# Hybrid encoder block on one Trainium2 core: latent attention takes its maxima over three PSUM banks at once and splits key tiles in pairs

## The chip, the cores and the metric

The kernel runs on 1 core of one Trainium2 chip. The metric is the device time of one execution in microseconds (us), median of the runs shown. Engines are called as in the profile: PE (matrix multiply) and PEld (its weight loads), ACT (ScalarE), DVE (VectorE), POOL (GpSimd), SP (issues most DMAs).

## What is computed

One encoder layer over two groups of 1040 tokens (1024 and 16 meta tokens), width 1024. Two attention mixers run in parallel on the same normed input: a grouped one (8 query heads, 2 key heads, 64 wide) and a latent one (8 heads, queries and keys 96 wide, values 64 wide). Their outputs are merged by sigmoid gates, then comes an expert-choice SwiGLU mixer. The part of the reference that the change touches:

```
def attend_mla(qb):
    qn, qr = qb[..., :MLA_NOPE_DIM], qb[..., MLA_NOPE_DIM:]
    s = (jnp.einsum('bqhd,bkhd->bhqk', qn, k_nope, preferred_element_type=jnp.float32)
         + jnp.einsum('bqhd,bkd->bhqk', qr, k_rope, preferred_element_type=jnp.float32)) * scale_m
    p = jax.nn.softmax(s, axis=-1).astype(v_m.dtype)
    o = jnp.einsum('bhqk,bkhd->bqhd', p, v_m)
...
mixed = (jax.nn.sigmoid(g_a) * jnp.matmul(o_g, w_o_gqa)
         + jax.nn.sigmoid(g_b) * jnp.matmul(o_m, w_o_mla))
h = h + jnp.matmul(mixed, w_out)
```

## The kernel before

The program is one fixed order of instructions per engine, held together by semaphores. Its stages follow one another: projections, grouped attention (`grouped_attention`), latent attention (`latent_attention`), `mix`, `residual`, choosing, experts. Every product is made of float32 operands split into a high part (a cast to float32r) and a low part (the value minus the cast), three matmuls per product.

Latent attention has 16 units (8 heads times 2 groups, unit n in program order). A unit is 3 blocks of 348, 348 and 344 queries, a block is 9 key tiles: eight of 128 keys and one of meta keys. That makes 48 blocks and 432 tiles, numbered t, with kk the tile inside its block. Per tile:

- PE, `scores(t)`: three matmuls into one of two banks of `n_st_ps` (lines 1872, 1873, 1876). Row 96 of the queries holds the maximum of each query and row 96 of the keys holds -1, so that the third matmul subtracts the maximum. The first tile of a block therefore waits in its third matmul for `row_done`.
- ACT, `exponential(t)` (L1929) writes `n_exps`, `hi(t)` (L1942, for meta keys L1937) casts it to `n_p_hi`.
- DVE, `lo(t)` (L2002, meta L1998) subtracts: `n_p_lo`.
- PE, `values(t)`: three matmuls into `n_o_ps` (L1893 to L1895), for meta keys one (L1889). They run LAG = 3 tiles behind the scores.

The maxima run ahead of all that. For each block 9 pieces are made: three chunks of 116 queries times three stretches of 348, 348 and 344 keys. A piece is one PE matmul (L1852) into one of three banks of `n_max_ps`, one DVE reduction (L1983) into `t_piece_max`; after the ninth, one or two small reductions (L1989) give `t_row_max`. One piece is issued per tile, 12 pieces ahead. In tile 7 of a block PE transposes the three columns of the next block's maxima into one row (`max_rows`, L1861), and ACT casts that row into the queries (`max_row`, L1947). ACT's order around a block's border is:

```
for t in range(NT + 1):
    if t < NT:
        exponential(t)
    if t >= 1:
        hi(t - 1)
    b, kk = tile_of(t)
    if kk == LAG + 1 and b >= 1:
        evacuate(b - 1)
    if kk == TILES - 1 and b + 1 < NB:
        max_row(b + 1)
```

When a block is finished, ACT copies its bank into `n_sums` (`evacuate`, L1957). When a unit is finished, POOL runs a chain on it: a DMA gathers the row of sums (`n_total`, L2037), DVE inverts it (`invert`, L2007, in DVE's order at tile 10 of the next unit), two DMAs spread the result (L2039, L2041), then POOL multiplies (L2043), casts (L2046) and subtracts (L2048) on 64 by 1040 elements, and two DMAs store to `o_t` (L2051). SP loads queries, keys and values of the next unit once the scores of the unit before are through; in the last unit SP waits for the store of unit 14 (`stored`), then loads the last token pieces and the first weights of `mix` (L301, L305, L308).

Between grouped and latent attention stand functions that the first leaves to the second in a dictionary `rest` (the last block's values on PE, its evacuation on ACT, its sum on DVE). POOL ends the grouped part with the scaling of its last two blocks (L1687 to L1701) and then sets row 96 of the keys with two memsets (L2029); PE waits for them (`ones_ready`) before the first scores. At the other border, `mix` begins with the cast of its first two weight pieces (ACT L2188), their subtraction (DVE L2239) and then matmuls (L2168, L2175); its SP part waits for the last unit's store (`attended["stored"]`) after the second pair of pieces.

## Time and profile before

| | before |
|---|---|
| median of 3 runs | 3044.73 us (3035.55 to 3045.96) |
| profiled execution, its own time | 3038.07 us |
| its span, first to last instruction | 3036.0 us |
| PE busy, share of the span | 2811.9 us, 93% |
| DVE busy | 1915.6 us, 63% |
| ACT busy | 1481.9 us, 49% |
| POOL busy | 628.7 us, 21% |
| mean granted PE clock | 0.968 |
| latent attention: first and last scores matmul (L1876) start | 895.8 and 1448.8 us |

A row of the time view reads: start in us, duration in us, engine, line, operation, output and inputs with shapes, count of merged instructions, and in brackets the idle time before and what ended it. Matmuls overlap: one row lasts about 0.32 us while the next starts some 0.16 us after it. Durations of groups are in ns.

### The profile page before, as it was taken

How to read it: one execution, taken by the hardware profiler on the slowest of the kernel's cores; microseconds unless marked ns; L12 is line 12 of the kernel's file. 1: busy time of each engine (PE TensorE's matmuls, PEld its weight loads, DVE VectorE, ACT ScalarE, POOL GpSimd, SP SyncE). 2: the span in 40 equal slices, each digit the busy share in tenths (PEclk: the TensorE clock that was granted, in tenths of full speed). 3: DMA queues.
4: the chain of work that ended last, by engine and by line, in shares of the span. 5: the costliest groups of instructions: out<-in, count | busy, mean ns of one | idle time of the engine just before them, and what ended most of it. 6: DMA issues, size and time to landing. Idle time of an engine off the chain costs nothing. (4 is left out here: it accounts for less than half of the span.)

```text
span 3036.0 us, 55157 instructions
## 1 busy us (share of the span) xinstructions
PE 2811.9 (93%) x19748; PEld 2615.8 (86%) x19748; DVE 1915.6 (63%) x3430; ACT 1481.9 (49%) x2813; POOL 628.7 (21%) x847
## 2 busy tenths in 40 slices
PE   8999899999989899999799999999973999999994
PEld 7888698999978788887799999988863999999994
DVE  6777667888878888888333434433335555555565
ACT  4333337888867676667322223322112445445453
POOL 0000113444431322223100000000004233333331
PEclk9999899999999999999999999999986999999997
DMA  6555592202223333452848484556646888899877
GB/s 210 159 158 181 174 370 65 71 22 71 50 45 78 86 90 88 96 141 71 252 124 243 111 242 127 146 167 188 195 128 154 191 202 200 205 207 209 196 173 263
DMA packets 534415, 466.66 MB, mean 154 GB/s; under 512 B 61906, under 2 KB 467106, under 8 KB 534256
## 3 DMA queue, kind: packets, MB, share of 16 engines
q1 hardware_dynamic: 510768, 403.68, 46.9%
q0 software_dynamic: 21120, 60.81, 9.1%
q8 instruction: 87, 1.43, 0.2%
q14 instruction: 72, 0.59, 0.1%
q10 hardware_dynamic: 2368, 0.16, 0.0%
HBM read 320.29 MB, written 144.21 MB: 153 GB/s over the span
## 5 line engine op out<-in xcount | busy, mean ns | idle before, releaser
L2168 PE MATMUL c_acc<-c_tokens,c_w_hi 128*128 128x260 f32 x2048 | 373.3, 284 | 13.1 <-DVE c_w_lo L2239 11.5
L2168 PEld LDWEIGHTS c_acc<-c_tokens,c_w_hi 128*128 128x128 f32 x2048 | 316.9, 189 | 13.5 <-issue 11.7
L2769 PE MATMUL e_gu<-e_x_hi,w_hi 128*128 128x260 f32 x1024 | 293.6, 287 | 0.9 <-DVE e_x_lo L2974 0.9
L2168 PE MATMUL c_acc<-c_tokens,c_w_lo 128*128 128x260 f32 x1024 | 289.8, 283 | 0.0
L2769 PE MATMUL e_gu<-e_x_lo,w_hi 128*128 128x260 f32 x1024 | 289.7, 283 | 0.0
L2239 DVE TENSOR_TENSOR c_w_lo<-c_raw,c_w_hi 128x1536 fp32r<-128x1536 f32 x64 | 114.5, 1790 | 277.4 <-ACT c_w_hi L2188 277.4
L2769 PE MATMUL e_gu<-e_x_hi,w_lo 128*128 128x260 f32 x1024 | 289.5, 283 | 0.0
L1929 ACT ACTIVATE n_exps<-n_st_ps 128x348 f32<-128x348 f32 (+3 forms) x432 | 198.8, 460 | 167.5 <-PE n_st_ps L1876 165.3
L2969 DVE TENSOR_TENSOR w_lo<-w_raw,w_hi 128x2048 fp32r<-128x2048 f32 x90 | 206.4, 2293 | 102.1 <-ACT w_hi L2870 101.3
L2002 DVE TENSOR_TENSOR n_p_lo<-n_exps,n_p_hi 128x348 fp32r<-128x348 f32 (+1 forms) x384 | 240.4, 626 | 38.0 <-ACT n_p_hi L1942 28.7
L1983 DVE TENSOR_REDUCE t_piece_max<-n_max_ps 116x1 f32<-116x348 f32 (+3 forms) x432 | 219.9, 511 | 41.3 <-PE n_max_ps L1852 39.7
L2188 ACT CAST c_w_hi<-c_raw 128x1536 fp32r<-128x1536 f32 x64 | 94.8, 1480 | 264.9 <-DMA c_raw<-in_w_o_gqa 228.4
L2769 PEld LDWEIGHTS e_gu<-e_x_hi,w_hi 128*128 128x128 f32 x1024 | 193.6, 189 | 1.1 <-DVE e_x_lo L2974 1.1
L2769 PEld LDWEIGHTS e_gu<-e_x_lo,w_hi 128*128 128x128 f32 x1024 | 193.7, 189 | 0.0
L2168 PEld LDWEIGHTS c_acc<-c_tokens,c_w_lo 128*128 128x128 f32 x1024 | 193.7, 189 | 0.0
L2769 PEld LDWEIGHTS e_gu<-e_x_hi,w_lo 128*128 128x128 f32 x1024 | 193.4, 189 | 0.0
L2175 PE MATMUL c_acc<-c_tokens,c_w_hi 128*128 128x260 f32 x1024 | 187.2, 283 | 0.0
L1942 ACT CAST n_p_hi<-n_exps 128x348 fp32r<-128x348 f32 (+1 forms) x384 | 181.3, 472 | 0.0
L2870 ACT CAST w_hi<-w_raw 128x2048 fp32r<-128x2048 f32 x90 | 171.2, 1902 | 8.9 <-PE e_dn L2794 7.5
L3110 POOL DMA_INDIRECT h_rows<-e_y,e_rows_out x60 | 104.9, 1748 | 333.2 <-DVE e_y L2996 319.4
L1576 DVE TENSOR_REDUCE t_peak<-t_s_ps 128x1 f32<-128x1024 f32 x132 | 160.6, 1217 | 19.7 <-PE t_s_ps L1390 19.4
L1601 DVE TENSOR_TENSOR t_pt_lo<-t_tp,t_pt_hi 128x512 fp32r<-128x512 f32 (+1 forms) x264 | 166.5, 670 | 2.3 <-ACT t_pt_hi L1522 2.0
(338 smaller groups left out, 7835.9 us busy)
## 6 DMA issues: line engine op xcount, KB each, us to landing
c_raw<-in_w_in SPq DMA_DIRECT2D x64, 512.0 KB, 5.4
w_raw<-in_w_gate SPq DMA_DIRECT2D x64, 512.0 KB, 6.7
w_raw<-in_w_up SPq DMA_DIRECT2D x64, 512.0 KB, 8.2
w_raw<-in_w_down SPq DMA_DIRECT2D x64, 512.0 KB, 4.7
c_tokens<-hn_t SPq DMA_DIRECT2D x16, 1040.0 KB, 8.9
c_tokens<-o_t SPq DMA_DIRECT2D x32, 520.0 KB, 6.7
r_mt<-mix_t SPq DMA_DIRECT2D x32, 512.0 KB, 5.2
mix_t<-c_out_hi SPq DMA_DIRECT2D x32, 260.0 KB, 2.1
```

Of the source, the lines that this page charges most:

```text
L1576: dve.tensor_reduce(peak[0:r, b % 2, i:i + 1], s_ps[0:r, n % 2, :], AX_X, ALU.max).then_inc(peak_done, 1)
L1601: dve.tensor_tensor(pt_lo[span], tp[:, f % RING, :].rearrange("p (t n) -> p t n", t=4)[:, :, 0:r], pt_hi[span].bitcast(F32), ALU.subtract) ...
L1929: act.activation(exps[0:r, t % EXPS, 0:w], st_ps[0:r, t % 2, 0:w], ACT.Exp).then_inc(exp_done, 1)
L1942: act.copy(p_hi[:, ring_slot(t), 0:w], exps[:, t % EXPS, 0:w]).then_inc(hi_done, 1)
L1983: dve.tensor_reduce(piece_max[0:r, b % 2, c, j:j + 1], max_ps[0:r, n % MAXES, 0:WIDTHS[j]], AX_X, ALU.max)\
L2002: dve.tensor_tensor(p_lo[:, at, 0:w], exps[:, t % EXPS, 0:w], p_hi[:, at, 0:w].bitcast(F32), ALU.subtract)\
L2168: pe.matmul(acc[:, b, mixer, 0:W], w[:, parity, mixer, k, :], tokens[t % 2][:, part, k, cols], start=(k == 0 and at == 0), stop=(k == DK - ...
L2175: ins = pe.matmul(acc[:, b, 2 + mixer, 0:W], w[:, parity, mixer, DK + k, :], tokens[t % 2][:, part, DK + mixer * OK + k, cols], start=(k = ...
L2239: dve.tensor_tensor(w_lo[:, parity, mixer, :, :], raw[:, mixer, :, :], w_hi[:, parity, mixer, :, :].bitcast(F32), ALU.subtract).then_inc(p ...
L2769: ins = pe.matmul(gu[:, j % 2, a, 0:W], w[:, j, at:at + P], t[:, k, :], start=(k == 0 and q == 0), stop=(k == DK - 1 and q == 2))
L2870: act.copy(w_hi[:, j, :], raw[:, j % RAW, :]).then_inc(slab_hi, 1)
L2969: dve.tensor_tensor(w_lo[:, j, :], raw[:, j % RAW, :], w_hi[:, j, :].bitcast(F32), ALU.subtract)\
```

## The change

In `latent_attention`:

- Maxima: each chunk of 116 queries is one step. Three matmuls of 348 keys (stretches from 0, 346 and 692, overlapping by two keys) fill the three banks, and one DVE reduction over 116 x 3 x 348 elements writes `t_row_max` directly. `t_piece_max` and the small reductions are gone. The next chunk's matmuls wait until the reduction before is done. The steps stand at fixed tiles: chunk 0 of block b+2 in tile 7 of block b, chunks 1 and 2 of block b+1 in tiles 1 and 3.
- The transposes of the maxima move from tile 7 to tile 6, and ACT's cast of the row from behind tile 8's exponential and tile 7's cast to directly behind tile 7's exponential.
- The cast to the high part and the subtraction handle two key tiles at once (128 x 2 x 348); the meta tile stays alone. The rings hold three pairs (before: six tiles of `n_p_hi` and four of `n_exps`).
- LAG is 5. `evacuate` stands at tile 5, without a cast beside it, and `invert` at tile 7 of the next unit.
- Border to grouped attention: the first block's chunks of maxima stand between the parts of the last grouped values; POOL's memsets stand ahead of the last grouped scaling; ACT's first row cast stands behind the last grouped evacuation.
- Border to `mix`: the last unit's inversion stands behind the subtraction of the first two weight pieces.

The diff, cut:

```diff
@@ grouped_attention @@
-            def finish():
-                for part in PARTS:
-                    values(BLOCKS - 1, part)
-                scale_rows(BLOCKS - 1)
-            rest["tensor"] = finish
+            rest["tensor"] = lambda part: values(BLOCKS - 1, part)
+            rest["parts"] = PARTS
+            rest["scale_rows"] = lambda: scale_rows(BLOCKS - 1)
...
-            for b in (BLOCKS - 2, BLOCKS - 1):
-                scale(b)
-                split_hi(b)
-                split_lo(b)
+            def finish():
+                for b in (BLOCKS - 2, BLOCKS - 1):
+                    scale(b)
+                    split_hi(b)
+                    split_lo(b)
+            rest["gpsimd"] = finish
@@ latent_attention @@
-    AHEAD, LAG = 12, 3
-    MAXES, RING, EXPS = 3, 6, 4
+    LAG = 5
+    PAIRS = XCH // 2
+    GROUPS_OF = PAIRS + 1
+    RING, EXPS = 3, 3
+    MAXIMA_AT = {7: (2, 0), 1: (1, 1), 3: (1, 2)}
...
-                if n >= MAXES:
-                    pe.wait_ge(max_done, n - MAXES + 1)
-                pe.matmul(max_ps[0:r, n % MAXES, 0:WIDTHS[j]], q[p][0:QK_M, at:at + r],
-                          k[0:QK_M, p, 0, STARTS[j]:STARTS[j] + WIDTHS[j]], start=True, stop=True).then_inc(max_filled, 1)
+                at_least(pe, max_done, 3 * b + c)
+                for j in range(3):
+                    ins = pe.matmul(max_ps[0:r, j, 0:WIDE], q[p][0:QK_M, at:at + r],
+                                    k[0:QK_M, p, 0, KEY_STARTS[j]:KEY_STARTS[j] + WIDE], start=True, stop=True)
+                ins.then_inc(max_filled, 1)
...
-            for n in range(9):
-                maxima(n)
-            grouped["rest"]["tensor"]()
-            for n in range(9, AHEAD):
-                maxima(n)
+            for c, part in enumerate(grouped["rest"]["parts"]):
+                maxima(0, c)
+                grouped["rest"]["tensor"](part)
+            grouped["rest"]["scale_rows"]()
+            maxima(1, 0)
             max_rows(0)
...
                     scores(t)
-                    if t + AHEAD < NT:
-                        maxima(t + AHEAD)
-                    if kk == TILES - 2 and b + 1 < NB:
+                    for ahead, c in chunks_at(t):
+                        maxima(ahead, c)
+                    if kk == 6 and b + 1 < NB:
                         max_rows(b + 1)
...
-                act.copy(p_hi[:, ring_slot(t), 0:w], exps[:, t % EXPS, 0:w]).then_inc(hi_done, 1)
+                act.copy(p_hi[:, ring_slot(t)[0], :, 0:w], exps[:, group % EXPS, :, 0:w]).then_inc(hi_done, 1)
...
-            for t in range(NT + 1):
-                if t < NT:
-                    exponential(t)
-                if t >= 1:
-                    hi(t - 1)
-                b, kk = tile_of(t)
-                if kk == LAG + 1 and b >= 1:
-                    evacuate(b - 1)
-                if kk == TILES - 1 and b + 1 < NB:
-                    max_row(b + 1)
+            for t in range(NT):
+                b, kk = tile_of(t)
+                exponential(t)
+                if kk == 7 and b + 1 < NB:
+                    max_row(b + 1)
+                if kk >= 2 and kk % 2 == 0:
+                    hi(t - 1)
+                if kk == 0 and b >= 1:
+                    hi(t - 1)
+                if kk == LAG and b >= 1:
+                    evacuate(b - 1)
+            hi(NT - 1)
...
-                dve.tensor_reduce(piece_max[0:r, b % 2, c, j:j + 1], max_ps[0:r, n % MAXES, 0:WIDTHS[j]], AX_X, ALU.max)\
-                    .then_inc(max_done, 1)
+                dve.tensor_reduce(row_max[0:r, b % 2, c:c + 1], max_ps[0:r, :, 0:WIDE], AX_XY, ALU.max).then_inc(max_done, 1)
...
+            for t in range(NT):
+                b, kk = tile_of(t)
+                for ahead, c in chunks_at(t):
+                    peaks(ahead, c)
+                if kk >= 2 and kk % 2 == 0:
+                    lo(t - 1)
+                if kk == 0 and b >= 1:
+                    lo(t - 1)
+                if b % BLOCKS == 0 and kk == 7 and b >= BLOCKS:
+                    invert(b // BLOCKS - 1)
+            lo(NT - 1)
...
                 pool.wait_ge(ones_ready[0], held.PREPARED + 1 + p)
+            grouped["rest"]["gpsimd"]()
             for landed, value in grouped["stored"]:
@@ mix @@
             split_pieces(0, 0, 0)
+            attended["invert_last"](dve)
```

How the change moves the instructions, at three places. First ACT around the border between two blocks inside latent attention (`t_q1_2440` are the queries with their row of maxima). Before:

```order
L1929 ACTIVATE n_exps<-n_st_ps 128x348
L1942 CAST n_p_hi<-n_exps 128x348
L1929 ACTIVATE n_exps<-n_st_ps 80x348
L1942 CAST n_p_hi<-n_exps 128x348
L1947 CAST t_q1_2440<-n_row_ps 1x348
L1929 ACTIVATE n_exps<-n_st_ps 128x348
L1937 CAST n_p_meta<-n_exps 80x348
```

and now:

```order
L1963 CAST n_p_hi<-n_exps 128x696
L1949 ACTIVATE n_exps<-n_st_ps 128x348
L1968 CAST t_q1_2440<-n_row_ps 1x348
L1949 ACTIVATE n_exps<-n_st_ps 80x348
L1963 CAST n_p_hi<-n_exps 128x696
L1949 ACTIVATE n_exps<-n_st_ps 128x348
L1958 CAST n_p_meta<-n_exps 80x348
```

The cast of the row stood behind the exponential of the block's last tile (80x348) and one more cast; it now stands ahead of both.

Second, DVE over one block that holds a unit's inversion, with the last meta subtraction of the block before as first row. Now:

```order
L2017 TENSOR_TENSOR n_p_meta<-n_exps,n_p_meta 16x344
L2008 TENSOR_REDUCE t_row_max<-n_max_ps 116x1
L2021 TENSOR_TENSOR n_p_lo<-n_exps,n_p_hi 128x696
L2008 TENSOR_REDUCE t_row_max<-n_max_ps 116x1
L2021 TENSOR_TENSOR n_p_lo<-n_exps,n_p_hi 128x696 x2
L2008 TENSOR_REDUCE t_row_max<-n_max_ps 116x1
L2026 RECIPROCAL n_inverse<-n_total 65x16
L2021 TENSOR_TENSOR n_p_lo<-n_exps,n_p_hi 128x696
L2017 TENSOR_TENSOR n_p_meta<-n_exps,n_p_meta 16x348
```

Before, a block had nine reductions of 116x348 and eight subtractions of 128x348 in turn, and the inversion stood one block later than here, behind the first subtraction:

```order
L1998 TENSOR_TENSOR n_p_meta<-n_exps,n_p_meta 16x348
L1983 TENSOR_REDUCE t_piece_max<-n_max_ps 116x1
L2002 TENSOR_TENSOR n_p_lo<-n_exps,n_p_hi 128x348
L2007 RECIPROCAL n_inverse<-n_total 65x16
L1983 TENSOR_REDUCE t_piece_max<-n_max_ps 116x1
```

Third, POOL at the border between the two attentions. Before, the memsets of `t_k` close the grouped scaling:

```order
L1687 TENSOR_TENSOR t_summed<-t_summed,t_scales 64x320
L1696 CAST t_out_hi<-t_summed 64x320
L1701 TENSOR_TENSOR t_out_lo<-t_summed,t_out_hi 64x320
L2024 UNCONDITIONAL_BRANCH
L2029 MEMSET t_k 1x1040 x2
```

and now they stand ahead of the scaling of the last two blocks:

```order
L2044 UNCONDITIONAL_BRANCH
L2049 MEMSET t_k 1x1040 x2
L1685 TENSOR_TENSOR t_summed<-t_summed,t_scales 64x384
L1694 CAST t_out_hi<-t_summed 64x384
L1699 TENSOR_TENSOR t_out_lo<-t_summed,t_out_hi 64x384
L1685 TENSOR_TENSOR t_summed<-t_summed,t_scales 64x320
```

## Rows read from the trace of the kernel before

**Rows 1.** One line's instructions (L1876): count, min/median/max ns, first and last start

```profile
L1876 PE MATMUL n_st_ps<-t_q,t_k x432: 316/323/493, 895.8 to 1448.8; 97*128 97x348 f32 x96, 97*128 97x344 f32 x48
```

**Rows 2.** Order of time, PE, a tile without a wait and the transposes

```profile
1201.76 0.32 PE L1872 MATMUL n_st_ps<-t_q,t_k 96*128 96x344 f32 x1
...
1202.85 0.32 PE L1872 MATMUL n_st_ps<-t_q,t_k 96*128 96x344 f32 x1
...
1203.32 0.32 PE L1852 MATMUL n_max_ps<-t_k,t_q 96*116 96x348 f32 x1
...
1203.71 0.39 PE L1893 MATMUL n_o_ps<-n_p_hi,t_v 128*65 128x344 f32 x1
```

**Rows 3.** Order of time, PE, two block borders that follow each other

```profile
1099.94 0.43 PE L1876 MATMUL n_st_ps<-t_q,t_k 97*128 97x348 f32 x1 [0.43 <-ACT t_q L1947]
...
1110.68 0.42 PE L1876 MATMUL n_st_ps<-t_q,t_k 97*128 97x348 f32 x1 [0.43 <-ACT t_q L1947]
```

**Rows 4.** Order of time, DVE, POOL and PE while POOL finishes a unit

```profile
1119.52 2.73 DVE L2002 TENSOR_TENSOR n_p_lo<-n_exps,n_p_hi 128x348 fp32r<-128x348 f32 x1 [0.18 <-ACT n_p_hi L1942]
...
1123.25 2.59 POOL L2048 TENSOR_TENSOR n_o_lo<-n_sums,n_o_hi 64x1040 fp32r<-64x1040 f32 x1
...
1124.01 2.21 DVE L1998 TENSOR_TENSOR n_p_meta<-n_exps,n_p_meta 16x348 fp32r<-16x348 f32 x1
...
1126.27 0.37 PE L1889 MATMUL n_o_ps<-n_p_meta,t_v 80*65 80x348 f32 x1 [1.34 <-DVE n_p_meta L1998]
```

**Rows 5.** The page's groups: busy us, mean ns of one, idle before

```profile
L2239 DVE TENSOR_TENSOR c_w_lo<-c_raw,c_w_hi 128x1536 fp32r<-128x1536 f32 x64 | 114.5, 1790 | 277.4 <-ACT c_w_hi L2188 277.4
...
L2002 DVE TENSOR_TENSOR n_p_lo<-n_exps,n_p_hi 128x348 fp32r<-128x348 f32 (+1 forms) x384 | 240.4, 626 | 38.0 <-ACT n_p_hi L1942 28.7
...
L2188 ACT CAST c_w_hi<-c_raw 128x1536 fp32r<-128x1536 f32 x64 | 94.8, 1480 | 264.9 <-DMA c_raw<-in_w_o_gqa 228.4
...
L1576 DVE TENSOR_REDUCE t_peak<-t_s_ps 128x1 f32<-128x1024 f32 x132 | 160.6, 1217 | 19.7 <-PE t_s_ps L1390 19.4
```

**Rows 6.** Order of time, border from grouped to latent attention

```profile
881.19 2.76 PE L1852 MATMUL n_max_ps<-t_k,t_q 96*116 96x348 f32 x6 [0.84 <-DVE t_piece_max L1983]
...
889.07 0.44 ACT L1947 CAST t_q<-n_row_ps 1x348 fp32r<-1x348 f32 x1 [8.52 <-PE n_row_ps L1861]
...
893.03 1.98 POOL L2029 MEMSET t_k<- 1x1040 f32 x2
...
895.06 0.66 PE L1872 MATMUL n_st_ps<-t_q,t_k 96*128 96x348 f32 x1 [6.03 <-POOL t_k L2029]
```

**Rows 7.** Order of time, from the last unit's first scores to the first matmul of mix

```profile
1416.60 0.33 PE L1872 MATMUL n_st_ps<-t_q,t_k 96*128 96x348 f32 x1
...
1423.60 0.55 POOL L2037 DMA_DIRECT2D n_total<-n_sums  x1 [11.22 <-ACT n_sums L1957]
...
1431.67 0.54 POOL L2039 DMA_DIRECT2D inverse_t<-n_inverse  x1 [7.52 <-DVE n_inverse L2007]
...
1448.40 2.08 SPq L301 DMA_DIRECT2D c_tokens<-o_t  x4
...
1463.00 0.77 PE L2168 MATMUL c_acc<-c_tokens,c_w_hi 128*128 128x260 f32 x2 [11.50 <-DVE c_w_lo L2239]
```

**Rows 8.** One tile's instructions (`n_total`): its DMA from issue to landing

```profile
DMA to landing us min/median/max: 2.4/3.5/5.2
```

**Rows 9.** Order of time, DVE, SP, ACT and PE in the first passes of mix

```profile
1457.46 0.25 DVE L2007 RECIPROCAL n_inverse<-n_total 65x16 f32<-65x16 f32 x1 [6.38 <-DMA n_total<-n_sums]
...
1477.45 1.30 SPq L301 DMA_DIRECT2D c_tokens<-hn_t  x2
...
1486.02 0.41 SPq L305 DMA_DIRECT2D c_raw<-in_w_in  x1
...
1494.46 1.48 ACT L2188 CAST c_w_hi<-c_raw 128x1536 fp32r<-128x1536 f32 x1 [9.94 <-DMA c_raw<-in_w_o_gqa]
...
1501.09 0.50 PE L2168 MATMUL c_acc<-c_tokens,c_w_hi 128*128 128x260 f32 x2 [1.56 <-DVE c_prod L2245]
```

More of the change, by code:

```diff
@@ L1760, in chunk, with groups_until, pair_before, group_end @@
         return cols.start + c * ROWS, r
[L1762 to L1764 removed]
+    def groups_until(t):
+        b, kk = tile_of(t)
+        return GROUPS_OF * b + kk // 2
     def ring_slot(t):
         b, kk = tile_of(t)
[L1769 to L1771 removed]
+        return (PAIRS * b + kk // 2) % RING, kk % 2
+    def pair_before(t):
         b, kk = tile_of(t)
[L1774 to L1775 removed]
+        x = PAIRS * b + kk // 2 - RING
+        return None if x < 0 else TILES * (x // PAIRS) + 2 * (x % PAIRS) + 1
+    def group_end(g):
+        b, j = g // GROUPS_OF, g % GROUPS_OF
+        return TILES * b + min(2 * j + 1, XCH)
+    def chunks_at(t):
+        b, kk = tile_of(t)
+        if kk in MAXIMA_AT:
+            ahead, c = MAXIMA_AT[kk]
+            if b + ahead < NB:
+                return [(b + ahead, c)]
+        return []
     with ExitStack() as ctx:
@@ L1784, in latent_attention @@
         q, k, v = held.q, held.k, held.v
[L1785 removed]
+        row_max = held.row_max
         sums = sb("sums", [VD + 1, 2, TOK])
```

101 lines of the change are left out of this document (42 added, 59 removed).

## The prediction, written before the changed kernel ran

> **What bounds the kernel now.** I read the page's forty slices first: PE is busy nearly throughout, and latent attention is a stretch in which it is a little less so, while DVE is at its highest there. Next the instructions of the scores line: 432 tiles between 895.8 and 1448.8, 1.283 us each [rows 1], so a block of nine tiles takes 11.55 us. Then the time view for what a tile must cost: between two first score matmuls with seven matmuls and no wait lie 1.09 us, 0.156 each [rows 2]. A block has 61 matmuls (27 scores, 9 maxima, 25 values), 9.55 us. The transposes of the maxima push the next value matmul from 0.16 to 0.39 us behind, 0.23 more [rows 2]. So **PE needs 9.8 us a block** and takes 11.55: 1.75 us are waits. Two quiet block borders that follow each other stand 10.74 us apart, and at each the third score matmul waited for ACT's cast of the row of maxima [rows 3]. That puts **about 0.95 us a block on this one wait** (0.43 idle by the row, the rest in the weight load held up with it and in the refill of the pipe). Units of three blocks really take (1416.60 - 895.06) / 15 = 34.8 us [rows 6, 7] against 3 x 10.74 = 32.2: **2.6 us a unit** are something else. Rows 4 show what: while POOL multiplies and subtracts 64 by 1040 elements, DVE's subtractions last 2.73 and 2.21 us, even one of 16 partitions, and the value matmul waits.
>
> **Part 1: the row of maxima comes early.** ACT now casts it behind tile 7's exponential. The exponential of tile 8 and a cast stood ahead of it before, and the first scores needed it one tile later; now there are over 1.5 tiles. The 0.95 us go if nothing on the new path is late, so I time a block, starting at its first score matmul, with tiles of 0.94 us (six matmuls), 0.47 more for the maxima in tiles 1, 3 and 7, and the transposes in tile 6. Results of a matmul are there some 0.2 us after the next could start. Durations: a pair's subtraction lies between one single and the 1536-wide one, 1790 ns [rows 5]. Less 696 against 1536 elements at DVE's 1.04 ns each (the 1024-wide reduction, 1217 ns, fits that slope) gives **0.9 us**. A three-bank reduction is the 1024-wide one plus 20 elements, **1.24 us** [rows 5]. A pair's cast is 1480 ns [rows 5] less 840 elements, between 0.67 (all proportional) and 0.94; I take 0.77.
> - Tiles 0 and 1: scores of tile 2 end at 2.8, ACT's exponential and pair cast at 4.15, DVE's subtraction at 5.05; the values want it at 5.8. Spare 0.75.
> - Chunk 1's maxima leave PE at 1.9, its reduction waits for DVE until 2.2 and ends at 3.4; PE wants the banks at 3.8. Spare 0.4. Chunk 2's reduction ends at 6.25, the transposes want it at 6.75. Spare 0.5.
> - Pairs 2-3, 4-5, 6-7 have 1.0 to 1.4 spare, the meta tile 3.
> - DVE's sum is 3 x 1.24 + 4 x 0.9 + 0.5 (a single one by the same slope) = 7.8 us, ACT's 12 of at most 0.46 (its 348-wide cast of the row: 0.44 [rows 6]) and 4 of 0.77, 8.6 us, both below 9.8.
>
> The nine small PE matmuls of maxima cost the same in threes; two keys more per chunk are nothing. Nine waits and eight small reductions that go cost nothing now, since DVE is not the bound; the cover is PE. **Gain 3 x 0.95 = 2.9 us in each of the 15 units that end before the last one starts: 43 us.**
>
> **Part 2: POOL's hold on DVE stays.** The unit's POOL work, some 6.3 us from about 1119.5 to 1125.84 [rows 4], is unchanged. By the timetable the first long one meets pair 4-5, which has 1.4 us spare and is late by little. The second meets pair 6-7, with up to 2.6 us to sit out against 1.1 spare: 1.5 us, then 0.7 at the next maxima, whose banks DVE frees late. That is 2.2 us, with 2.6 before by the sum above. LAG = 5 gives longer cover, but a pair is two tiles late at once. **I count 0.** From below: all 2.6 x 15 = 39 us gained, if the cover holds. From above: see the third rival. `invert` now stands where DVE may arrive before the data. The last block's copy ends some 7 us into a unit (its DMA starts at 1423.60, 7.0 after the unit's 1416.60 [rows 7]), its DMA lands 3.5 later, 2.4 to 5.2 [rows 8], so at 9.4 to 12.2; DVE is there at 10.2. The pair queued behind it is ready at 10.7 and has 1.1 spare, so the median costs nothing and the slowest landing about 1 us. The chain behind it starts some 3.5 us sooner: 11.3 us into the unit against 1431.67 - 1416.60 less POOL's 0.3, 14.8.
>
> **Part 3: the first border.** Scores start at 895.06 because POOL's memsets end the grouped scaling [rows 6]. Ahead of the scaling they wait only for the last grouped scores, and are done long before the 889 that comes next. Next in line is ACT's row of maxima, 889.07 to 889.5 before, and the 2.76 us in which PE ran six maxima against DVE's reductions [rows 6] shrink as values fill them. With the reductions of 1.24 us each still felt once or twice, I get first scores at 887: **8 us gained**. At least 5.5 (row as late as before), at most 9.
>
> **Part 4: the last border.** Mix starts when unit 14 is stored: 1431.67 to 1448.40 is 16.7 us, and from there weights, cast and subtraction take 14.6 to 1463.00 [rows 7]. Both stay. With the inversion 3.5 us sooner in the unit, mix starts 3.5 us sooner counted from the last unit's start, **3.5 us gained**; PE just idles longer there, since the unit's own blocks are faster too. But the last inversion now comes behind the first two weight subtractions, 2.5 us after mix's start instead of 5.5 before it (1457.46) [rows 9]. SP stands behind that store with the next tokens and the third pair of pieces: store seen 20 us after the inversion (1477.45), pieces issued at 1486.02, cast at 1494.46, PE already waits 1.56 at 1501.09 [rows 9]. In the new order the store is seen 19.5 to 22.5 after mix's start instead of 14.5. SP waited anyway some 3 us for the first output in between. So the third pieces come 2 to 5 us later: **3.6 us lost**.
>
> **Sum.** 43 + 0 + 8 + 3.5 - 3.6 = 51 us. Everything behind mix follows PE and its own weights, and moves along. The profiled execution took 3038.07 us, which becomes 2987; it lay 6.7 below the median 3044.73, which becomes **2994**.
>
> **A page that speaks against it.** Rows 4 show DVE held for most of a POOL instruction. The Trainium skill, page "SBUF — State Buffer", section "Who interferes with whom", says that a VectorE instruction with two SBUF inputs and a GpSimd instruction that reads SBUF shut each other out for the whole instruction, the later one waiting. By that rule POOL's cast holds DVE too, and fewer, longer subtractions would be hit as hard as many short ones; the trace agrees for the two arithmetic ones (2.73 and 2.21), and its rows don't isolate the cast.
>
> **Rivals.**
> 1. *The cover holds* (0.20). PE's five tiles of lag and a DVE that is busy 7.8 of 9.8 us hide POOL too. For it: three of four pairs have 1 us or more spare. Against: up to 2.6 us to sit out. It gives 51 + 25 to 39, median 2955 to 2969.
> 2. *A new short wait in each block* (0.17). The three places with 0.4 to 0.75 spare are each gone if crossing the third bank costs DVE some 0.3 us or the pair cast takes its upper bound of 0.94, and PE waits for DVE instead of ACT. It would take 0.5 to 0.9 us a block back: 24 to 43 us, median 3018 to 3037. For it: single semaphore hops are not in my timetable. Against: the 1024-wide reduction crosses two banks at 1217 [rows 5].
> 3. *POOL's work stands on PE in full* (0.07), slower. All of POOL's 6.3 us a unit end up as PE waits, because a held pair delays the reduction behind it, that the single-buffered banks, and those the transposes, each long hold with another 0.7. It costs 7.7 us a unit instead of 2.6, 77 us in 15 units, and the sum turns to 26 slower: 3071. It decides from 2.6 + 51/15 = 6 us a unit. Against: 1.1 to 1.4 us of each hold are covered by the timetable, and DVE got a subtraction through between POOL's instructions (2.73 from 1119.52, the next of 2.21 only from 1124.01 [rows 4]).
> 4. *The change doesn't reach PE* (0.06): the wait for the row is replaced by one for the exponentials, whose order on ACT got bursts of cast and copy (tiles 5 to 8 hold 4.2 us of ACT work against 4.5 of PE). Then only the border's 8 us remain, 3037.
>
> **Chances.** The forecast has 0.50, and 2975 to 3015 as its own range. The range takes in rival 1 and most of rival 2: **2960 to 3030**. It leaves out the ends of rival 1 and 2, and rivals 3 and 4. A measurement of this kernel tells some 0.5%, 15 us, from no change. Faster by more: forecast, rival 1, most of rival 2, 0.83. Within: the rest of rival 2 and rival 4, 0.10. Slower: 0.07.
>
> **What would show it.** Right: scores from about 887; 10 us between block borders in quiet stretches; no PE wait on `t_q`; single waits of PE for `n_p_lo` and `n_max_ps`, 2 to 3 us a unit; unit starts 32 us apart; pair subtractions of 0.9 us, up to 3.4 under POOL; reductions of 1.24; an idle PE of some 12 to 14 us ahead of mix, and a wait of 4 to 7 us for its third pieces. Wrong: PE waits in every block for `t_row_max` or `n_p_lo` (rival 2), for ACT's `n_exps` (rival 4), or units still 35 us apart.

## The result

| | before | after |
|---|---|---|
| median | 3042.47 us (3035.55 to 3047.84, 8 runs) | 3019.0 us (3007.32 to 3030.13, 8 runs) |
| ratio | | 0.9923 [0.9903, 0.9943] |
| profiled execution, its own time | 3038.07 us | 3020.98 us |
| its span | 3036.0 us | 3018.7 us |
| latent attention: last unit's first scores minus first scores | 521.5 us | 508.9 us |
| mean granted PE clock of the span | 0.968 | 0.965 |

The change gives 23 us by the medians, 17.3 by the two spans, and not the forecast 51: the time is inside the range of 2960 to 3030, 25 us above the 2994. In the profiles the 17.3 split up as follows, each from the start of a row (units count from 0, so U15 is the last one; "mix" is the first matmul of the output mix):

| stretch | before | after | gained | forecast |
|---|---|---|---|---|
| up to the first scores | 895.06 | 885.63 | 9.4 | 8 |
| first scores to U15 | 521.5 | 508.9 | 12.6 | 43 + 0 |
| U15 to mix | 46.4 | 42.7 | 3.7 | 3.5 |
| mix to the end | 1573.0 | 1581.4 | -8.4 | -3.6 |

So the first border and the start of the mix did about what was forecast. Most of the missing gain is in the second row (30.4 us), a smaller part in the fourth (4.8).

### The profile page after: what moved, and what is told of

Same layout as the page of the kernel before. It is cut to its first block and busy times, and to the rows that moved or that the text cites. A ratio compares the mean times of both kernels' runs of the same rounds, so it can differ in the third digit from the quotient of the medians.

```text
span 3018.7 us, 53994 instructions
## 1 busy us (share of the span) xinstructions
PE 2810.1 (93%) x19748; PEld 2624.4 (87%) x19748; DVE 1857.1 (62%) x2886; ACT 1452.7 (48%) x2621; POOL 633.6 (21%) x847
## 5 line engine op out<-in xcount | busy, mean ns | idle before, releaser
L2189 PE MATMUL c_acc<-c_tokens,c_w_hi 128*128 128x260 f32 x2048 | 375.2, 285 | 17.5 <-DVE c_w_lo L2260 9.2
L2021 DVE TENSOR_TENSOR n_p_lo<-n_exps,n_p_hi 128x696 fp32r<-128x696 f32 (+1 forms) x192 | 214.2, 1117 | 105.3 <-ACT n_p_hi L1963 104.4
L2008 DVE TENSOR_REDUCE t_row_max<-n_max_ps 116x1 f32<-116x1044 f32 x144 | 178.6, 1241 | 11.5 <-PE n_max_ps L1869 9.7
```

What stands on the lines that cost most here:

```text
L2008: dve.tensor_reduce(row_max[0:r, b % 2, c:c + 1], max_ps[0:r, :, 0:WIDE], AX_XY, ALU.max).then_inc(max_done, 1)
L2021: dve.tensor_tensor(p_lo[:, at, :, 0:w], exps[:, group % EXPS, :, 0:w], p_hi[:, at, :, 0:w].bitcast(F32), ALU.subtract).then_inc(lo_done, 1)
L2189: pe.matmul(acc[:, b, mixer, 0:W], w[:, parity, mixer, k, :], tokens[t % 2][:, part, k, cols], start=(k == 0 and at == 0), stop=(k == DK - ...
```

## The profile after

The single instructions take about what was forecast. The scores line (L1894) waits for ACT's row of maxima 2 times in all, 0.7 us. The weights' subtraction in the mix, the pairs' subtractions and the reductions have these groups on the page (busy us, mean ns of one, idle before; against [rows 5]):

```profile
L2260 DVE TENSOR_TENSOR c_w_lo<-c_raw,c_w_hi 128x1536 fp32r<-128x1536 f32 x64 | 112.6, 1759 | 290.9 <-ACT c_w_hi L2209 290.9
...
L2021 DVE TENSOR_TENSOR n_p_lo<-n_exps,n_p_hi 128x696 fp32r<-128x696 f32 (+1 forms) x192 | 214.2, 1117 | 105.3 <-ACT n_p_hi L1963 104.4
...
L2008 DVE TENSOR_REDUCE t_row_max<-n_max_ps 116x1 f32<-116x1044 f32 x144 | 178.6, 1241 | 11.5 <-PE n_max_ps L1869 9.7
```

The three-bank reduction takes 1241 ns as forecast (1.24). A pair's subtraction has a mean of 1117 ns, with 880 for an undisturbed one (below): the rest is time in which POOL held it.

Order of time after, the border into latent attention, against [rows 6]: the memsets are early, and the first scores matmul waits for nothing any more.

```profile
876.89 1.98 POOL L2049 MEMSET t_k<- 1x1040 f32 x2
...
885.63 0.40 PE L1890 MATMUL n_st_ps<-t_q,t_k 96*128 96x348 f32 x1
```

The windows view shows where a unit's time goes. The rows are two quiet blocks and the third of unit 4, a quiet one and the third of unit 6, and the third of unit 9, each from its first scores (L1890) to the next block's: length, busy us of each engine with instructions, granted PE clock (as a share of 2.4 GHz), DMA share and GB/s.

```profile
1029.01:1039.04 10.03, 10.03 (x67) 9.36 (x65) 7.50 (x9) 7.52 (x17) 0.56 (x1) 1.00 0.73 162
1039.04:1049.08 10.04, 10.04 (x66) 9.37 (x65) 7.86 (x9) 7.52 (x17) 3.37 (x3) 1.00 0.30 83
1049.08:1065.17 16.09, 13.82 (x66) 11.62 (x65) 11.89 (x10) 7.85 (x17) 5.30 (x5) 0.79 0.14 33
...
1112.64:1122.68 10.04, 10.04 (x66) 9.34 (x65) 7.71 (x10) 7.52 (x17) 2.49 (x3) 1.00 0.29 83
1122.68:1133.78 11.10, 10.23 (x66) 9.30 (x65) 9.62 (x9) 7.46 (x17) 6.79 (x5) 1.00 0.20 49
...
1220.68:1234.37 13.69, 10.92 (x66) 9.16 (x65) 11.93 (x10) 7.64 (x17) 5.79 (x5) 1.00 0.16 40
```

A quiet block takes 10.04 us and PE is busy in all of it. Before it took 10.74 [rows 3]: **0.70 gained per block, not 0.95**. The third block, in which POOL finishes the unit before, is longer, and by very different amounts. In unit 6 it takes 11.10. In unit 4 it takes 16.09: PE idles 2.27 us, and its busy time is 3.8 us longer for the same matmuls, at a mean granted clock of 0.79. From 1055.67 on, behind the first two waits, PE ran at the lower level, 1.2 GHz, for 6.8 us, at half speed 3.4 us lost. In unit 9 PE idles even longer, 2.77 us, but keeps the full clock, and the block takes 13.69. Of units 1 to 8 six have a third block of 14.9 to 16.6 us, units 6 and 8 and the later ones 11.1 to 13.7. Before, those of units 1 to 14 took 12.5 to 14.7. So the wait of 2.2 us a unit in the forecast was right for a unit like 4; the lower clock that came with it was missing.

Order of time, DVE then POOL then PE, in unit 4's long block:

```profile
1047.37 2.60 DVE L2021 TENSOR_TENSOR n_p_lo<-n_exps,n_p_hi 128x696 fp32r<-128x696 f32 x1 [0.83 <-ACT n_p_hi L1963]
1049.89 1.23 DVE L2008 TENSOR_REDUCE t_row_max<-n_max_ps 116x1 f32<-116x1044 f32 x1
1051.04 3.10 DVE L2021 TENSOR_TENSOR n_p_lo<-n_exps,n_p_hi 128x696 fp32r<-128x696 f32 x1
...
1046.78 2.44 POOL L2064 TENSOR_TENSOR n_sums<-n_sums,n_factor 64x1040 f32<-64x1040 f32 x1 [3.18 <-DMA n_factor<-inverse_t]
1049.29 1.59 POOL L2067 CAST n_o_hi<-n_sums 64x1040 fp32r<-64x1040 f32 x1
1050.95 2.45 POOL L2069 TENSOR_TENSOR n_o_lo<-n_sums,n_o_hi 64x1040 fp32r<-64x1040 f32 x1
...
1050.02 0.38 PE L1911 MATMUL n_o_ps<-n_p_hi,t_v 128*65 128x348 f32 x1 [0.30 <-DVE n_p_lo L2021]
1054.20 0.38 PE L1911 MATMUL n_o_ps<-n_p_hi,t_v 128*65 128x348 f32 x1 [1.31 <-DVE n_p_lo L2021]
1056.02 1.22 PE L1869 MATMUL n_max_ps<-t_k,t_q 96*116 96x348 f32 x3 [0.66 <-DVE t_row_max L2008]
```

Both arithmetic instructions of POOL start just before a pair's subtraction (0.6 and 0.1 us), which then ends 0.75 us behind POOL's end. The reduction between them is not touched. PE's three waits of 0.30, 1.31 and 0.66 us follow at once. In unit 6 the order is another:

```profile
1120.97 0.88 DVE L2021 TENSOR_TENSOR n_p_lo<-n_exps,n_p_hi 128x696 fp32r<-128x696 f32 x1 [0.83 <-ACT n_p_hi L1963]
1121.77 1.24 DVE L2008 TENSOR_REDUCE t_row_max<-n_max_ps 116x1 f32<-116x1044 f32 x1
1123.56 1.36 DVE L2021 TENSOR_TENSOR n_p_lo<-n_exps,n_p_hi 128x696 fp32r<-128x696 f32 x1 [0.55 <-ACT n_p_hi L1963]
1124.94 1.25 DVE L2017 TENSOR_TENSOR n_p_meta<-n_exps,n_p_meta 16x348 fp32r<-16x348 f32 x1
1126.23 1.25 DVE L2008 TENSOR_REDUCE t_row_max<-n_max_ps 116x1 f32<-116x1044 f32 x1
1127.50 1.73 DVE L2021 TENSOR_TENSOR n_p_lo<-n_exps,n_p_hi 128x688 fp32r<-128x688 f32 x1
...
1121.26 2.91 POOL L2064 TENSOR_TENSOR n_sums<-n_sums,n_factor 64x1040 f32<-64x1040 f32 x1 [3.00 <-DMA n_factor<-inverse_t]
1124.24 1.59 POOL L2067 CAST n_o_hi<-n_sums 64x1040 fp32r<-64x1040 f32 x1
1125.90 2.60 POOL L2069 TENSOR_TENSOR n_o_lo<-n_sums,n_o_hi 64x1040 fp32r<-64x1040 f32 x1
```

POOL's multiplication starts 0.29 behind a subtraction and is itself the one that waits (2.91 for 2.44); most of it then lies beside a reduction, which reads PSUM and takes its usual 1.24. The cast holds too: the subtraction of 16 partitions behind it takes 1.25 for its usual 0.51, and the cast itself 1.59, since the subtraction ahead reaches 0.68 into it; the cast of the last unit in the kernel before, with no subtraction beside it, takes 1.06. The longest hold on a pair is 0.85 us.

The two kinds lie close together. Counted from the third block's start, the multiplication starts 1.86 us ahead in unit 5 and 1.85 in unit 7 (0.13 to 0.14 ahead of the subtraction of pair 4-5: 16.59 and 15.11 us), and 1.42 and 1.44 in units 6 and 8 (0.28 to 0.29 behind it: 11.10 and 11.09).

Waits in the stretch from the first scores to U15 (engine, line, released by: us in total, times, longest):

```profile
PE n_o_ps L1911 <- DVE n_p_lo L2021: 14.8, 16, 1.3
PE n_max_ps L1869 <- DVE t_row_max L2008: 13.6, 19, 1.8
DVE n_inverse L2026 <- DMA n_total<-n_sums: 10.2, 14, 1.6
...
PE n_max_ps L1869 <- DMA t_k<-kr_t: 4.4, 1, 4.4
```

The last two were not there before in this form. DVE now stands for the landing sums 14 times. And PE waits once for the second unit's keys (`t_k`), at 907.57, because it needs them sooner while SP still issues them behind the last stores of grouped attention. That block takes 16.35 us.

The mix, order of time in DVE, SP, ACT and PE, against [rows 9]:

```profile
1439.68 0.24 DVE L1998 RECIPROCAL n_inverse<-n_total 65x16 f32<-65x16 f32 x1
...
1459.13 1.47 SPq L301 DMA_DIRECT2D c_tokens<-hn_t  x2
...
1466.24 2.69 SPq L308 DMA_DIRECT2D c_raw<-in_w_o_gqa  x1
...
1475.14 1.47 ACT L2209 CAST c_w_hi<-c_raw 128x1536 fp32r<-128x1536 f32 x1 [16.24 <-DMA c_raw<-in_w_o_gqa]
...
1481.77 0.80 PE L2189 MATMUL c_acc<-c_tokens,c_w_hi 128*128 128x260 f32 x2 [7.86 <-DVE c_prod L2266]
```

The inversion stands 2.4 us behind mix's start (1437.26), SP sees the store 19.4 later, and PE waits 7.86 us for the third pieces' product where it waited 1.56. The forecast had 3.6 for this. The idle time alone grew by 6.3. In addition PE is at the lower clock (1.2 GHz) from 1478.92 to 1485.75, 42 us into the mix, where before it keeps the full clock; 4.0 us of that lie behind the wait and cost some 2.0. The two make up the 8.4.

## The experiments

Theory A: POOL's holds on DVE's subtractions are what makes third blocks long, and they cost more than before, because PE now drops to its lower clock more often. Against it stand the ring of exponentials, the width of the pair's subtraction, and waits that the wider instructions make among themselves. Each kernel was measured beside the kernel before; the changed kernel, run again, gave 3016.47 us.

> The changed kernel itself, as the yardstick on this chip. It should again take 0.990 to 0.994 of the kernel before (about 3019 us), with quiet blocks of 10.0 us in the attention of the second kind and third blocks of 15 to 16.6 us in most of its first eight units.

Measured: ratio 0.9912 [0.9892, 0.9932]. Third blocks are 15 to 16.1 us in units 1 to 4, 7, 9 and 11, else 11.1 to 12.3. The program is the same, but unit 5 is now short (11.1) and units 9 and 11 are long, as a difference of 0.4 us between the two kinds lets one expect. The sum of the third blocks is the same, 198.2 and 198.4 us.

**Without POOL's holds**, in the changed kernel and in the one before:

```diff
-pool.tensor_tensor(sums[0:VD, p, :], sums[0:VD, p, :], factor[:, :], ALU.mult)
+pool.tensor_tensor(sums[0:VD, p, 0:16], sums[0:VD, p, 0:16], factor[:, 0:16], ALU.mult)
...
```

The cast and the subtraction are cut in the same way, and the two output tiles are filled with zeros once. The scaling of the other 1024 columns is left out.

> The changed kernel with GpSimd's multiplication, cast and subtraction of a finished unit cut from 1040 columns to 16; the scaling of the other 1024 columns of the latent outputs is left out. Theory A (GpSimd's holds of about 2.5 us each on VectorE's subtractions are what makes every third block long, and in the changed kernel they cost more than before, because VectorE, a ring of three pairs and one set of maxima banks leave less slack): all blocks fall to the quiet 10.04 us, the excess of 57 us over units 0 to 14 shrinks to the 5 to 10 that the late keys of the second unit cost, and the whole falls by 45 to 52 us against the changed kernel. Theory B (the lost 20 us come from TensorE's half clock, whatever the holds, or from waits that the wider instructions make among themselves): third blocks stay over 11 us in several units and the whole falls by less than 35 us.

> The kernel before with the same three GpSimd instructions cut to 16 columns; the scaling of the other 1024 columns of the latent outputs is left out. Theory A: blocks fall to the quiet 10.74 us, which gives 35 to 38 us (the excess of before over units 0 to 14), so that this pair of kernels differs by about 10 us more than the pair with the whole GpSimd work, some 35 us. Theory B: the pair without GpSimd's work differs by the same 17 to 23 us as the pair with it.

Measured: 2960.33 us (0.9733 [0.9714, 0.9752]) and 2991.57 us (0.9835 [0.9817, 0.9853]). That is 56 us less than the changed kernel and 50 less than the one before. The waits of PE (and of its weight load PEld) in the same stretch, first without POOL's work in the changed kernel, then in the one before:

```profile
PE n_max_ps L1870 <- DMA t_k<-kr_t: 5.0, 1, 5.0
PE n_max_ps L1870 <- DVE t_row_max L2009: 1.9, 5, 0.5
```

```profile
PEld n_st_ps L1877 <- ACT t_q L1948: 31.2, 44, 0.7
...
PE n_st_ps L1877 <- ACT t_q L1948: 18.6, 44, 0.4
```

Theory A stands. All 14 third blocks are at 9.98 to 9.99 in the one and 10.59 to 10.67 in the other, and the waits of PE for `n_p_lo` are gone; between the first scores and U15 the lower clock is left in unit 0 alone. The third blocks together lost 48.5 us in the changed kernel and 39.3 in the one before: that is what the holds cost there. The rest of the 56 and 50 us, more than either expectation had, comes mainly from U15 on, where POOL's work on the last units is gone too (11.9 and 7.0 us). The pair now differs by 31 us instead of 23 to 26. That also tells what the row of maxima was worth: the second fence has all of its cost, 44 waits of 0.71 us in the weight load, and 0.70 a block is the difference of two quiet blocks. The tile with the wait takes 1.81 us where one with the same seven matmuls takes 1.11 to 1.13, again 0.7. The forecast's further 0.25 us are not there.

**The second unit's keys first.**

```diff
-            grouped["rest"]["sync"]()
             for n in range(N_UNITS):
...
                     held.load_qk(sp, scr, u + 1)
+                    if n == 0:
+                        grouped["rest"]["sync"]()
```

> The changed kernel with SyncE's loads of the second unit's queries and keys issued ahead of the last outputs of the first kind of heads, instead of behind them. Theory: the wait of TensorE of 4.4 us for these keys in unit 0 goes, and with it the 6.8 us at half clock that follow: 4 to 8 us less than the changed kernel. Rival: the stores that are now later hold GpSimd's start, or the keys were not what TensorE waited for: within 2 us of the changed kernel.

Measured: 3009.28 us, 7.2 less than the changed kernel on the same chip (0.9901 [0.9875, 0.9927]; the intervals of the two overlap). The profile is plainer: unit 0 takes 29.2 us instead of 36.1, its wait on `t_k` and its half clock are gone. The place and the 6.8 us in the profile are shown; that the medians differ by nearly as much could be chance, since the third blocks also fell differently (8.4 us less in all).

**The last inversion ahead of mix's first subtractions.**

```diff
-            split_pieces(0, 0, 0)
             attended["invert_last"](dve)
+            split_pieces(0, 0, 0)
```

> The changed kernel with VectorE's last inversion ahead of its first subtractions of weights in the mix, instead of behind them. Theory: the inversion runs as soon as its sums land, about 2 us sooner than the 1439.68 of the changed kernel or more, GpSimd's scaling, its stores, SyncE's tokens and the third pieces of the weights follow, TensorE's wait of 7.9 us on the mix's products and the 6.8 us at half clock behind it shrink: mix to end falls from 1581.4 towards 1573, 5 to 8 us less in all. Rival: TensorE's first weights of the mix are what decides, and they come later by the wait for the sums (3.5 us): no gain or up to 3 us more.

Order of time of this kernel:

```profile
1439.16 0.25 DVE L1998 RECIPROCAL n_inverse<-n_total 65x16 f32<-65x16 f32 x1 [6.57 <-DMA n_total<-n_sums]
...
1444.65 0.77 PE L2189 MATMUL c_acc<-c_tokens,c_w_hi 128*128 128x260 f32 x2 [11.24 <-DVE c_w_lo L2260]
...
1481.89 0.50 PE L2189 MATMUL c_acc<-c_tokens,c_w_hi 128*128 128x260 f32 x2 [0.31 <-DVE c_prod L2266]
```

Measured: 3010.21 us (0.9895 [0.9879, 0.9911]), 6 to 9 less. PE's wait on `c_prod` falls from 7.86 to 0.31, the low clock 42 us into the mix is gone, and mix to end takes 1572.5 instead of 1581.4. Mix itself starts 43.6 after U15 instead of 42.7, so the rival's price is under 1 us. The order of these two steps costs the change some 8 us (8.9 less 0.9).

**Four groups of exponentials instead of three** (`RING, EXPS = 3, 4`).

> The changed kernel with four groups of exponentials in the ring instead of three. Theory A1 (the ring of three groups is what turns GpSimd's hold on VectorE into TensorE's idle time: ScalarE's exponentials wait 21.8 us for VectorE's subtractions): the bad third blocks fall from 15 to 16.6 us to 12 to 13 and the whole by 15 to 25 us. Theory A2 (the values and the maxima wait for VectorE in any case, TensorE's own two waits of 17.6 and 13.6 us): less than 5 us.

Measured: 3025.61 us (0.9947 [0.9929, 0.9965]), 7 to 9 more than the changed kernel. No gain. ACT's waits for `n_p_lo`, 20.7 us before, are gone from the list, but PE's own remain, 12.1 us for `n_p_lo` and 14.0 for `t_row_max`. Five third blocks still take 13.7 to 16.1 us. Theory A1 falls: the wait at the ring was a symptom.

**Single subtractions, paired casts.**

```diff
-                dve.tensor_tensor(p_lo[:, at, :, 0:w], exps[:, group % EXPS, :, 0:w], ...
+                for which in range(2):
+                    dve.tensor_tensor(p_lo[:, at, which, 0:w], exps[:, group % EXPS, which, 0:w], ...
```

> The changed kernel with VectorE's subtractions of one key tile at a time again (two of 348 columns for one of 696), each signalled to TensorE by itself; casts stay paired. Theory B (the pair's subtraction, waited for as a whole, is what made third blocks worse than in the kernel before): they fall to the 12.5 to 14.7 of before and the whole by 8 to 15 us. Theory A (GpSimd's holds against VectorE's fill, whatever the width): VectorE has one instruction more per pair, quiet blocks stay at 10.0, third blocks at 13 to 16.6, and the whole is 0 to 10 us longer.

Measured: 3033.35 us (0.9974 [0.9962, 0.9986]), 14 to 17 us longer than the changed kernel, more than either expected. Theory B falls: finer subtractions don't help. PE waits for them less (2.6 us instead of 14.8) and for the maxima more:

```profile
PE n_max_ps L1869 <- DVE t_row_max L2008: 37.5, 26, 4.0
```

Two single subtractions take 1.04 us (0.52 each) where the pair's takes 0.88, and the reduction stands behind them in DVE's order; that this is why the maxima are later was not tested apart. Third blocks reach 17.7 us. The pair's subtraction is therefore a gain of its own here, of some 15 us, that the forecast had at nothing ("DVE is not the bound").

**POOL's work in quarters**, the same work in shorter holds:

```diff
-pool.tensor_tensor(sums[0:VD, p, :], sums[0:VD, p, :], factor[:, :], ALU.mult).then_inc(out_chain, 1)
+for part in PIECES:
+    ins = pool.tensor_tensor(sums[0:VD, p, part], sums[0:VD, p, part], factor[:, part], ALU.mult)
+ins.then_inc(out_chain, 1)
```

> The changed kernel with each of GpSimd's three instructions of a unit split into four of 260 columns, the same work in all. Theory A (one hold of about 2.5 us is what stalls VectorE for longer than the rings carry): a hold is 0.7 to 0.9 us, third blocks come to 11 to 13 us, and the whole is 10 to 25 us shorter. Rival (what counts is the sum of time in which GpSimd and VectorE are at the memory together, not the length of one hold): third blocks stay as they are, within 4 us of the changed kernel.

> The kernel before with GpSimd's three instructions in quarters. Theory A: its third blocks fall from 12.5 to 14.7 us to 10.8 to 11.3, 25 to 35 us less than before, near 3010; against the changed kernel in quarters (2987.57) the change is then worth 20 to 28 us. If long holds hurt only the changed kernel: within 10 us of before.

Measured: 2987.57 us (0.9824 [0.9811, 0.9838]) with the change and 3005.09 us (0.9877 [0.9854, 0.9899]) without. POOL's groups, changed kernel over 900 to 1380 us, then its quarters (busy us, mean ns | idle):

```profile
L2064 POOL TENSOR_TENSOR n_sums<-n_sums,n_factor 64x1040 f32<-64x1040 f32 x13 | 33.4, 2566 | 46.4 <-DMA n_factor<-inverse_t 46.4
L2069 POOL TENSOR_TENSOR n_o_lo<-n_sums,n_o_hi 64x1040 fp32r<-64x1040 f32 x13 | 32.2, 2474 | 1.0
```

```profile
L2066 POOL TENSOR_TENSOR n_sums<-n_sums,n_factor 64x260 f32<-64x260 f32 x60 | 55.9, 956 | 54.4 <-DMA n_factor<-inverse_t 54.4
L2075 POOL TENSOR_TENSOR n_o_lo<-n_sums,n_o_hi 64x260 fp32r<-64x260 f32 x60 | 54.4, 933 | 1.2
```

A multiplication now takes 4 x 956 ns = 3.8 us instead of 2.57, so POOL works longer in all. Yet third blocks fall to 10.0 to 10.6 us with the change and 10.6 to 11.3 without. The length of one hold decides, not their sum. The kernel before had the same kind of loss in it: quarters give it 35 us, against 29 to 31 in the changed one. Both kernels with quarters differ by 17.5 us and not by 31 as without POOL's work (20.7 and 30.0 by the profiles' spans). The profiles show where: from mix to the end this changed kernel takes 1586.5 and the one before 1574.7, 7.9 more apart than the pair without POOL's work, and from the first scores to U15 the quarters leave 4.6 us more in the changed kernel. The late keys are in the changed kernel of both pairs and explain nothing of it.

**The inversion three key tiles later**, so that all of POOL's work comes later in the unit:

```diff
-                if b % BLOCKS == 0 and kk == 7 and b >= BLOCKS:
+                if b % BLOCKS == 1 and kk == 1 and b >= BLOCKS:
```

> The changed kernel with VectorE's inversion of a finished unit three key tiles later (the second tile of the second block instead of the eighth of the first). The waits for the landing sums (10.2 us in 14 units) go. Theory P (which instruction of VectorE a hold meets decides whether a third block takes 11.1 or 15 to 16 us, so a shift of GpSimd's work by some 3 us changes the pattern over the units): good and bad units are others than 6, 8, 10 and 13 good, and the sum of third blocks moves by more than 10 us in either direction. Rival (bad units are bad by something else): the same units are good and bad, the whole within 10 us less.

Measured: 2998.97 us (0.9862 [0.9839, 0.9885]), 17.5 to 20 less. Third blocks are now 11.0 to 12.1 in all of units 1 to 14 (26 us less in all), none with half clock, and the waits for the landing sums are gone from second blocks (10.05 to 10.07, up to 11.1 in the changed kernel). One unit's long block, DVE, POOL and PE:

```profile
1034.56 1.24 DVE L2008 TENSOR_REDUCE t_row_max<-n_max_ps 116x1 f32<-116x1044 f32 x1
1036.34 1.88 DVE L2021 TENSOR_TENSOR n_p_lo<-n_exps,n_p_hi 128x696 fp32r<-128x696 f32 x1 [0.55 <-ACT n_p_hi L1963]
1038.25 1.25 DVE L2017 TENSOR_TENSOR n_p_meta<-n_exps,n_p_meta 16x348 fp32r<-16x348 f32 x1
...
1035.02 2.45 POOL L2064 TENSOR_TENSOR n_sums<-n_sums,n_factor 64x1040 f32<-64x1040 f32 x1 [3.04 <-DMA n_factor<-inverse_t]
1037.54 1.59 POOL L2067 CAST n_o_hi<-n_sums 64x1040 fp32r<-64x1040 f32 x1
...
1040.83 0.74 PE L1869 MATMUL n_max_ps<-t_k,t_q 96*116 96x348 f32 x3 [1.39 <-DVE t_row_max L2008]
```

The first 0.8 us of the multiplication now lie beside a reduction, and the cast meets the subtraction of 16 partitions (1.25 for 0.51). What is left is one wait of 1.39 us for the maxima. Theory P holds: the same POOL instructions cost 1.5 us a unit in this place, where they cost 3.4 in the changed kernel.

**Together.** The first has quarters, keys first and inversion before mix; the second eighths instead of quarters; the third is the first with the later inversion; the fourth is the third with POOL's instructions whole.

> Three edits of the earlier runs together on the changed kernel: GpSimd's three instructions of a unit in quarters (alone 29 us less), the last inversion ahead of the mix's first subtractions (alone 6 to 9 us less), the second unit's loads ahead of the last stores of the first kind (alone 7 us less). If they are three separate places, the sum is about 44 us less than the changed kernel: 2970 to 2978. If they share a cause (the half clock in unit 0 or the phase of GpSimd's work), the sum falls short: over 2980.

> The same with GpSimd's instructions in eighths of 130 columns. Theory (the length of one hold decides, and 0.95 us is still more than VectorE's slack in a pair of key tiles): third blocks fall from 10.2 to 10.6 us to under 10.2 and the whole by 2 to 6 us more. Rival (at a quarter the holds are already hidden and only GpSimd's own time grows, from 9.4 us in a unit): within 2 us of the version in quarters.

> Four edits together: quarters, the inversion ahead of the mix's subtractions, the second unit's loads first, and the inversion of finished units three key tiles later. If VectorE's wait for landing sums is what lengthens second blocks to 10.3 to 12.2 us in the version without the last edit (2974.24), they fall to 10.07 and the whole is 6 to 12 us shorter. If the later GpSimd work meets what the earlier did not (the last block of a unit, the mix), the two cancel: within 3 us of 2974.

> The same without quarters: GpSimd's three long instructions as in the changed kernel, but later by three key tiles, with the loads and the last inversion moved. This tells whether the phase of long holds can do what shorter holds do. Theory: third blocks of 11.5 us as in the run with the later inversion alone, against 10.2 to 10.5 with quarters: 10 to 16 us longer than with quarters, 2976 to 2984. Rival (the phase slips with the earlier start, since in the loads-first run the pattern of units changed): third blocks of 13 us and more in several units, over 2990.

| | us | ratio to before | first scores to U15 | U15 to mix | mix to end |
|---|---|---|---|---|---|
| changed kernel | 3019.0 | 0.9923 [0.9903, 0.9943] | 508.9 | 42.7 | 1581.4 |
| quarters, keys, inversion | 2974.24 | 0.9778 [0.9758, 0.9797] | 461.9 | 46.1 | 1576.3 |
| the same in eighths | 2979.55 | 0.9791 [0.9771, 0.9812] | 466.8 | 50.5 | 1575.5 |
| quarters and later inversion | 2972.17 | 0.9762 [0.9745, 0.9778] | 457.6 | 52.3 | 1574.4 |
| whole and later inversion | 2984.83 | 0.9801 [0.9785, 0.9818] | 475.4 | 46.1 | 1574.7 |

The gains add, nearly: 42 to 47 us under the changed kernel, and 66 to 70 under the kernel before. Shorter than a quarter gives nothing: POOL's own time grows (8 x 0.62 us for a multiplication). The 4.9 us by which the eighths are longer up to U15 are no sign against them, though: one block of unit 14 took 15.8 us, because DVE's inversion waited 3.35 us for its sums to land. With the later inversion the stretch to U15 is 4.4 us shorter, but U15 to mix grows by 6.2; the two versions can't be told apart by their times. With whole instructions in the later place third blocks are 11.4 to 13.3 us (one of them with some lower clock), and the time is 12.7 us longer than with quarters: place and length each give something. What is late next is in this row of the fastest one:

```profile
1396.62 0.77 PE L2197 MATMUL c_acc<-c_tokens,c_w_hi 128*128 128x260 f32 x2 [20.67 <-DVE c_w_lo L2268]
```

PE now idles 20.7 us ahead of the mix, since SP issues the mix's weights only behind the previous unit's store, and that store waits for POOL. How much of it could be had by loading the weights earlier was not tried.

## Why the prediction was partly wrong

- **The row of maxima** ("about 0.95 us a block on this one wait", 43 us): the mechanism was right, the size was not. The wait is gone, and a quiet block is 0.70 shorter, 45 x 0.70 = 31.5 us. That is 11.5 us of the missing 30.4. The step that failed is PE's need, put at 9.8 us a block where it is 10.04: 0.156 us a matmul came from one tile 344 wide, and quiet tiles 348 wide take 0.16; the transposes add 0.30 and not 0.23. Of 10.74 less 9.8 the forecast then ascribed what the idle row didn't have to "the weight load held up with it" and "the refill of the pipe". The weight load's waits, 44 of 0.71 us, had the whole number.
- **POOL's hold** ("I count 0"): the idle time was right, also in its working. In unit 4 the first long instruction meets pair 4-5 and costs 0.30 us, the second meets pair 6-7 and costs 1.31, the maxima behind it 0.66: 2.27 where the forecast had 2.2. Over the third blocks of units 1 to 14 PE idles 26.3 us, and before it idled 26.2 besides the wait for the row (32.2 - 14 x 0.43). The step that failed is that the sum priced idle time alone. In these blocks PE is at 1.2 GHz for 30.7 us, and was for 13.7 before; the 17.0 more are 8.5 us lost (an estimate, half of 17.0). All third blocks together lie 47.8 us over quiet ones, before 37.5. The profile of before had hints: its longest third blocks, 14.1 to 14.7, are those with a stretch at half clock.
- **The rest of the second row.** The excess of units 0 to 14 over three quiet blocks each is 38.2 us before (521.5 - 15 x 32.22) and 57.1 after (508.9 - 15 x 30.12), 18.9 more. Of these 10.3 are the third blocks, 6.3 the late keys, which the forecast didn't mention, and 3.8 the inversion's waits for its sums, less some 1.5 elsewhere. For these waits the forecast had nothing at the median and 1 us for the slowest, which is right (0.1 and 1.04), but it put their sum at nothing.
- **Which hold meets which instruction** was read off a timetable ("the first long one meets pair 4-5"). That is so in the long blocks; in units 6 and 8 POOL comes 0.4 us later, finds the subtraction running and waits itself. The timetable was not that fine.
- **The first border** (8 us): right, 9.4, of which 1.2 lie ahead of it: the first matmul of maxima starts at 878.4 instead of 879.6.
- **The last border** (+3.5, -3.6): the first half is right (42.7 for 42.9), though PE idles 9.2 us ahead of the mix and not 12 to 14. The second is mis-sized, 8.4 lost instead of 3.6; reversing the order of inversion and subtraction gave 8.9 back in the profile. The idle time grew by 6.3, and the lower clock behind the wait, some 2 us, was not in the sum.
- **Cover and fill of DVE** ("nine waits and eight small reductions that go cost nothing"): only true in quiet blocks. Splitting the subtractions again cost 14 to 17 us.
- **Rivals:** rival 3 had the chain of unit 4's waits (a held pair delays the reduction, that the banks), but not its price: 6.0 us over a quiet block in unit 4, not 7.7, and 1.1 in unit 6. Rival 2 has the measured time in its 3018 to 3037, which is luck, as is a time inside the range: no quiet block has a wait for DVE.
- The Trainium skill, page "SBUF — State Buffer", section "Who interferes with whom", says further that a VectorE reduction never contends with GpSimd on this chip, and that whoever issues first keeps the shared pair. The rows agree with both: reductions take 1.23 to 1.25 us beside POOL's work, the later subtraction waits in the long block (2.60 and 3.10), and the later multiplication in unit 6 (2.91). The subtraction of 1.36 us there started 0.61 us before the multiplication's end and waited for that. The cast, which the rows of before did not isolate, follows the rule too (1.25 for 0.51). Had the forecast used both sentences it would have asked for order, and not only for length.

Left open: why about the same idle time leads to more of the lower clock (unit 4 idles 2.27 us and has 6.8 us of it, unit 9 idles 2.77 and has none); and which part of the change, the faster blocks, the single set of maxima banks or the earlier inversion, moved the holds onto pair subtractions. The run with the later inversion shows that place is enough to undo most of it, not that it alone did it.

## What to carry to other kernels

A wait of PE has two prices: its idle time, and what the lower clock takes around and behind it. Here 2.3 us idle cost 6.0 in unit 4, while 2.8 without the lower clock cost 3.7 in unit 9. When an edit takes slack out of the engines around PE, look first for long instructions of one engine that hold another's, and cut them up: the same POOL work in four pieces took half as long again and gave 29 us. And when an early step of one stage is put behind the first step of the next, follow the chain that hangs on it to its end.
